# A decoder trunk on one core: the start's transfers divided between SyncE's and ScalarE's queues

## The reference

```python
c_act = jax.nn.silu(c)
for l in range(DEPTH):
    mod = c_act @ ada_w[l] + ada_b[l]
    sh1, sc1, g1, sh2, sc2, g2 = [t[:, None, :] for t in jnp.split(mod, 6, axis=-1)]
    h = rms_norm(x, norm_mix_w[l]) * (1.0 + sc1) + sh1
    proj = h @ w_in[l]
    ...            # window attention and mLSTM branches, gates, conv, merge
    x = x + g1 * (merged @ w_out[l])
    h2 = rms_norm(x, norm_ffn_w[l]) * (1.0 + sc2) + sh2
    x = x + g2 * grouped_moe(h2, router_w, router_bias, w_gate[l], w_up[l], w_down[l])
return x
```

## Time and profile before

| what | value |
|---|---|
| median of three executions | 1733.24 us |
| profiled execution, first to last instruction (span) | 1724.8 us |
| median less span (what lies around the span, and differences between executions) | 8.4 us |
| TensorE busy | 1506.9 us, 87% of the span |
| first matmul record | 11.38 us |
| head on TensorE | 18.40 to 44.06 us |
| last transfer of the head landed | 38.62 us |
| bytes moved | 366.59 MB, mean 213 GB/s |

### The profile page before, as it was taken

One profiled execution on the slowest core, in us unless ns is written; L12 is line 12 of the kernel. 1 busy time (PEld: TensorE's weight loads), 2 busy tenths in 40 slices (PEclk: granted clock), 3 DMA queues, 4 the chain that ended last, 5 costly groups with the idle time before them and its releaser, 6 DMA issues.

```text
span 1724.8 us, 18335 instructions
## 1 busy us (share of the span) xinstructions
PE 1506.9 (87%) x5819; PEld 669.3 (39%) x5820; DVE 563.9 (33%) x1459; ACT 323.4 (19%) x809; POOL 121.8 (7%) x157
## 2 busy tenths in 40 slices
PE   4999999999983999987749999999999387999982
PEld 1544444544441333332335444454444132333330
DVE  1346432446333212111134554243642411221213
ACT  3133411200011212111132343111000121221210
POOL 1100000011101000000111000000110100000001
PEclk8999999999996999999769999999999789999996
DMA  9822111055747899999952111113563799997984
GB/s 307 338 97 98 49 49 49 13 206 173 291 142 268 268 375 379 376 388 360 322 180 98 49 49 50 49 49 108 206 224 145 292 314 381 378 354 247 310 303 165
DMA packets 160813, 366.59 MB, mean 213 GB/s; under 512 B 12433, under 2 KB 14705, under 8 KB 160753
## 3 DMA queue, kind: packets, MB, share of 16 engines
q1 hardware_dynamic: 127568, 256.26, 42.2%
q0 software_dynamic: 21664, 83.89, 12.8%
q10 hardware_dynamic: 11520, 25.70, 5.0%
HBM read 334.37 MB, written 31.46 MB: 212 GB/s over the span
## 4 chain that ended last, share of the span: by engine, by line
PE 69%; DMA 11%; SPq 5%; DVE 5%; issue 4%; ACT 2%; POOL 2%; ACTq 0%; DVEq 0%; POOLq 0%; PEldq 0%
PE bank L939 23%; PE bank L1160 14%; PE bank L929 11%; PE bank L1105 6%; PE bank L1172 6%; DMA weight_ring<-in_w_up_dram 6%; DMA regA<-in_w_up_dram 2%; SPq L428 2%; SPq L431 2%; SPq L371 2%; DMA weight_ring<-in_ada_w_dram 1%; PE bank L1152 1%; PE bank L999 1%; POOL expert_rows L558 1%; PE bank L988 1%
## 5 line engine op out<-in xcount | busy, mean ns | idle before, releaser
L939 PE MATMUL bank<-h_features,weight_ring 128*128 128x512 f32 x768 | 342.4, 599 | 3.1 <-ACT regB L674 1.9
L1160 PE MATMUL bank<-weight_ring,merged_features 128*64 128x512 f32 x960 | 227.2, 628 | 35.3 <-DMA weight_ring<-in_w_up_dram 28.2
L939 PEld LDWEIGHTS bank<-h_features,weight_ring 128*128 128x128 f32 x768 | 144.8, 192 | 182.7 <-issue 182.4
L929 PE MATMUL bank<-weight_ring,h_features 128*128 128x512 f32 (+1 forms) x512 | 196.1, 541 | 1.7 <-ACT h_features L628 1.7
L1703 DVE TENSOR_TENSOR merged_features<-bank,merged_features 64x512 f32<-64x512 f32 x44 | 30.5, 693 | 381.8 <-ACT merged_features L809 381.8
L1160 PEld LDWEIGHTS bank<-weight_ring,merged_features 128*64 128x64 f32 x960 | 73.5, 144 | 165.4 <-issue 160.8
L929 PEld LDWEIGHTS bank<-weight_ring,h_features 128*128 128x128 f32 x512 | 96.0, 190 | 97.0 <-issue 91.6
L1160 PE MATMUL bank<-h_features,merged_features 128*64 128x512 f32 x256 | 117.1, 612 | 11.0 <-DMA regA<-in_w_up_dram 10.0
L1160 PE MATMUL bank<-regA,merged_features 128*64 128x512 f32 x256 | 117.5, 614 | 0.0
L1105 PE MATMUL bank<-weight_ring,merged_features 128*128 128x512 f32 x256 | 110.4, 593 | 3.0 <-POOL merged_features L538 3.0
L1172 PE MATMUL bank<-weight_ring,merged_features 128*64 128x512 f32 x480 | 109.6, 598 | 1.6 <-DVE merged_features L1689 1.6
(11 more groups left out here) (304 smaller groups left out, 1376.1 us busy)
## 6 DMA issues: line engine op xcount, KB each, us to landing
weight_ring<-in_ada_w_dram SPq DMA_DIRECT2D x24, 2048.0 KB, 8.7
weight_ring<-in_w_gate_dram SPq DMA_DIRECT2D x22, 2048.0 KB, 21.1
weight_ring<-in_w_down_dram POOLq DMA_DIRECT2D x22, 2048.0 KB, 14.9
weight_ring<-in_w_up_dram SPq DMA_DIRECT2D x22, 2048.0 KB, 20.4
weight_ring<-in_w_in_dram SPq DMA_DIRECT2D x18, 2048.0 KB, 8.9
h_features<-in_w_gate_dram SPq DMA_DIRECT2D x10, 2048.0 KB, 17.4
regA<-in_w_up_dram SPq DMA_DIRECT2D x10, 2048.0 KB, 27.4
regB<-in_w_down_dram POOLq DMA_DIRECT2D x10, 1536.0 KB, 11.5
```

The lines of the kernel that those rows point to most:

```text
L929: ins = te.matmul(bank[:, 0:w], hT[:, k, P * i:P * i + P], wv[:, k, :], start=(k == 0), stop=(k == KD - 1))
L939: ins = te.matmul(bank[:, :], wv[:, k, c0:c0 + P], rhs[:, k, :], start=(k == 0), stop=(k == kn - 1))
L1160: ins = te.matmul(ps[3][64 * part:64 * part + 64, :], xT[:, k, :], w[:, k, :], start=(k == 0), stop=(k == KD - 1))
```

## The change

SP issues `c`, the positions and then all four conditioning pieces in a row. The tokens, the router bias, the router matrix and the fourteen parameter transfers are issued by ScalarE, ahead of its first activation, in that order; the wait for `zeroed` goes with them. `params` now takes the engine as an argument; in the second layer's case SP issues them as before. Nothing that any engine waits for is changed, and no byte is added or removed.

```diff
+        def params(eng, l):
+
+            def rows(dst, src):
+                eng.dma_start(dst, src).then_inc(params_in, 16)
...
         @block.sync
         def _(sp):
-            def params(l):
...
             sp.dma_start(crow, c.rearrange("a (k p) -> (a k) p", p=P)).then_inc(const_in, 16)
             with nc.allow_non_contiguous_dma(reason="positions by token"):
                 sp.dma_start(rt[:, 0:NT].bitcast(I32), positions.rearrange("a (i p) -> p (a i)", p=P)).then_inc(const_in, 16)
-            sp.dma_start(rbias[:, :], router_bias.rearrange("(a e) -> a e", a=1).to_broadcast([P, E])).then_inc(const_in, 16)
-            load_item(sp, 0, 0, head_in[0])
-            sp.wait_ge(zeroed, 2)
-            sp.dma_start(rwz[:, :, 0:E], router_w.rearrange("(k p) e -> p k e", p=P)).then_inc(const_in, 16)
-            params(0)
-            sp.dma_start(xs[:, :, :], x.rearrange("a (i p) d -> p (a i) d", p=P)).then_inc(x_in, 16)
-            for n in range(1, HEAD):
+            for n in range(HEAD):
                 load_item(sp, 0, n, head_in[n])
...
                 with sp.If(l < DEPTH - 1):
-                    params(nxt)
+                    params(sp, nxt)
...
             ac = nc.scalar

+            act.dma_start(xs[:, :, :], x.rearrange("a (i p) d -> p (a i) d", p=P)).then_inc(x_in, 16)
+            act.dma_start(rbias[:, :], router_bias.rearrange("(a e) -> a e", a=1).to_broadcast([P, E])).then_inc(const_in, 16)
+            act.wait_ge(zeroed, 2)
+            act.dma_start(rwz[:, :, 0:E], router_w.rearrange("(k p) e -> p k e", p=P)).then_inc(const_in, 16)
+            params(act, 0)
             act.wait_ge(dve_const, 1)
```

More of the change, by code:

```diff
@@ L361, in share @@
             return cleared[n::5]
+        def params(eng, l):
+            def rows(dst, src):
+                eng.dma_start(dst, src).then_inc(params_in, 16)
+            rows(prm[0:8, :], lay(norm_mix_w, l).rearrange("a (k p) -> (a k) p", p=P))
+            rows(prm[8:16, :], lay(norm_ffn_w, l).rearrange("a (k p) -> (a k) p", p=P))
+            rows(prm[16:48, :], lay(conv_w, l).rearrange("a j (m p) -> (a j m) p", p=P))
+            rows(prm[48:56, :], lay(conv_b, l).rearrange("a (m p) -> (a m) p", p=P))
+            rows(prm[56:60, :], lay(mlstm_norm_w, l).rearrange("a (m p) -> (a m) p", p=P))
+            rows(prm[60:108, :], lay(ada_b, l).rearrange("a (m p) -> (a m) p", p=P))
+            rows(g1bc[:, :], lay(ada_b, l)[:, 2 * D:3 * D].to_broadcast([P, D]))
+            rows(wqk[:, 0, :], lay(q_norm_w, l).to_broadcast([P, HD]))
+            rows(wqk[:, 1, :], lay(k_norm_w, l).to_broadcast([P, HD]))
+            rows(sinkb[:, :], lay(sinks, l).to_broadcast([P, HQ]))
+            with nc.allow_non_contiguous_dma(reason="gate columns and biases"):
+                rows(gbias[0:4, :], lay(b_igate, l).rearrange("a h -> h a"))
+                rows(gbias[32:36, :], lay(b_fgate, l).rearrange("a h -> h a"))
+                rows(wgz[:, :, 0:4], cols8(w_in, l, MI, 4))
+                rows(wgz[:, :, 4:8], cols8(w_in, l, MF, 4))
         block = ctx.enter_context(nc.Block())
```

## The result

The changed kernel is slower, by less than forecast. Median 1735.12 us (1730.96 to 1739.41, 20 runs) against 1731.38 us (1725.11 to 1740.47, 20 runs) before; the ratio is 1.0024, with a 95% interval of 1.0013 to 1.0035. By the ratio that is +4.2 us (2.3 to 6.1) where +10.6 was forecast; the medians differ by 3.7. The time lies inside the stated range and the change has the forecast sign, but it is within the 0.3% that was to count as no change, and less than half of what was forecast. Of the 8.7 us between the forecast time (1743.8) and the median, 1.9 come from the kernel before, whose median of three was 1733.24. In what follows, one of the eight executions of experiment 4 is left out of every figure: it took 2701.77 us at a mean granted clock of 0.56.

The account below looks back on a forecast made before the run. Bound at the start by three paths ending together (pieces 1 and 3, token path), then dense TensorE work. Parameters at 34.3 plus a 20.35 us head end at 54.65 against 44.06: +10.6 on 1733.24 gives 1743.8 us, range 1729 to 1749.

Parts of the forecast that it names:

- Turns between queues: SP's and ScalarE's queues at the start: one packet each in turn, so 259 turns put parameters at 34.3 us; chance 0.62.
- The first phase: Start of the queues: `x` goes in turn with the positions' 4-byte packets, 5.5 us, and its packets are over at 7.9.
- The head's own time: TensorE from parameter transpose to last conditioning sum: dense from 34.3, 20.35 us, end at 54.65 against 44.06 before.
- Three paths that end together: Start of the kernel before: pieces 1 and 3 and the token path end together, then TensorE runs 12.76 us nearly without gap.
- ScalarE's hold: ScalarE held while issuing, let go at 24 us with about 105 packets per engine standing; hidden with 2 us to spare.
- Median less span: Whole kernel: the 8.4 us between profiled span and median time is carried along unchanged into the forecast.
- The chances: Whole kernel against a 0.3% (5.2 us) threshold: slower 0.64, same 0.31, faster 0.05.
- rival of small packets several to a turn: Queues at the start: 1.6 to 2.5 small packets per 2 KB piece, parameters at 26.4 to 21.6, +2.7 to -2.0 us; chance 0.24.
- n = 1.25: Small packets per 2 KB piece at about which the loss was said to pass 0.3%.
- rival of turns slower than their packets: Queues at the start: a turn takes 1.38 times its packets' time, +20 us, 1754 us; chance 0.05.

Follow-up runs that it names:

- experiment 4: Kernel before, but TensorE starts the head only when all four conditioning pieces have landed, transfers unchanged; 1739.34 us, ratio 1.0047 to the kernel before.
- experiment 6: Changed kernel, but SP issues the four conditioning pieces only when ScalarE's parameters have landed; 1734.34 us, ratio 1.0005 to the kernel before.
- experiment 3: Changed kernel, but SP issues the gate columns behind the four pieces, with their own count; 1732.87 us, ratio 1.0008 to the kernel before.
- experiment 1: Kernel before, but only `x` is issued from ScalarE, everything else stays with SP; 1729.48 us, ratio 0.9981 to the kernel before.
- experiment 2: Changed kernel, but `x` is issued by SP behind piece 0, only the small transfers by ScalarE; 1730.34 us, ratio 0.9980 to the kernel before.
- experiment 5: Kernel before, but TensorE repeats conditioning group 0 five times and group 2 twice, transfers unchanged; 1734.15 us, ratio 1.0007 to the kernel before.
- experiment 7: Changed kernel, but SP issues everything in one queue, gate columns, router bias and router matrix last with own counts; 1727.80 us, ratio 0.9974 to the kernel before.

## Why the prediction was right and wrong

**Turns between queues: right where it was needed.** Small packets of one queue and 2 KB packets of the other pass one for one, at 92 ns a pair where 94 were reckoned; predicted were parameters at 34.3 and the router matrix at 15.7, measured 35.5 and 17.4. Experiment 6 takes the neighbour away and the same transfers land 20 us earlier; experiment 3 takes 130 of the packets away and the head starts 11 us earlier. The first phase was read too simply: beside `x` the positions' 4-byte packets did not go in turn (12 of them passed with 197 of `x` between 4 and 6 us), and some still passed when `x` was over. The rest of the 1.2 and 1.7 us is not taken apart.

**The head's own time: wrong, and this is the step that failed.** "From 34.3 TensorE runs the head dense: ... 20.35 us". The mechanism, a dense head from the landing of the parameters, was right; its size was taken from rows at 1.2 GHz. It measured 13.3 us. The text had seen that the clock might be the higher one and priced that at 3.4 us less, from group 0's 3.21 us "at 1.00". That row was misread. The first clock record in the trace of the kernel before begins at 21.44 us, and ahead of it the column shows 1.00 for want of a record; group 0 ran from 18.81 to 22.02, mostly at the lower level, and a group at 2.4 GHz is 1.92. The terms add up: 10.6 + 1.2 (later parameters) - 7.0 (shorter head) is the +4.8 us measured at the head's end. Experiment 4 shows the short head without any change of transfers: 13.7 us.

**Three paths that end together: right,** and it has a second side. Before, TensorE stood about 5.7 us within the head, for pieces 1 and 3 and for ScalarE; these waits and the lower clock of most of its groups make the 12.3 us between 25.7 and 13.3. The late start of the changed kernel removes both, all but the first two groups' share. Experiment 3 shows that the paths stand close: with the parameters out of the way the first sum waits for ScalarE.

**ScalarE's hold: right in sign,** too long by 5 us, no cost. When ScalarE was let go at 18.7 us, 2308 of its packets were still to pass, 144 on each engine, where the estimate was 105.

**Median less span.** The 8.4 us stand alike in the time before and in the forecast time, so they did not touch the forecast change. One execution's time less its own span is 1.6 us (1737.23 less 1735.6; 1726.02 less 1724.4). The rest was that the profiled execution of before was a fast one.

**The chances.** 0.64 for slower by over 0.3% rested on the whole 10.6. With the head 7.0 us shorter the same sum gives +3.6, under the stated bound of 5.2 us, and "no change" would have been the likelier. The rival of small packets several to a turn, whose places were taken as mixed evidence, is refuted by 1733 to 1732 and by parameters at 35.5 where it had 21.6 to 26.4. Its turning point, n = 1.25, was a slip: by the prediction's own terms a loss of 5.2 us is reached at about n = 1.35. The rival of turns slower than their packets is refuted by the 92 ns a pair.

Open is why experiments 1, 2, 5 and 7 time 2.5 to 4 us better than the first projection of their one profile stands against the mean of before. For experiment 7 it is 1.9 us ahead, and 4.5 us (2.1 to 6.9) were measured; its last projection of the first layer starts at 441.77, only 0.2 us ahead of that mean. So the profile does not show where the timed gain of experiment 7 lies.

## What to carry to other kernels

In these runs a transfer of thousands of tiny pieces was cheap alone (about 10 ns a packet and engine) and dear beside 2 KB pieces (92 ns), because the two queues took turns by packets: moved to a queue of its own it landed later, and so did whatever waited for it. Of the two remedies tried, letting such transfers pass first and alone (experiment 6) came out level with the kernel before, and putting them behind everything that is waited for, with a count of their own (experiment 7), came out 0.3% ahead. When a wait goes or comes in front of TensorE, price the matmuls behind it at the clock they will have there, from rows at both levels, not at the one they had.

## What the runs showed of the hardware

- In the three profiles of the kernel before, one group of 16 matmul records of 512 columns, 32 rows each, takes 3.21 to 3.64 us at 1.2 GHz or mostly so, and 1.92 at 2.4 (second profile); a sum of eight one-column matmuls takes 1.86 and 1.05. In every head here the first groups take more than 1.92 us each.
- Waits of TensorE of 2.0, 2.5 and 2.8 us (experiments 5, 3 and 6) were followed by the lower level, waits of 1.8 and 1.9 us (experiments 7 and 6) by a group of 1.92. A shorter wait was no warrant: the third profile of before has 1.54 us and then a group of 3.32. What decides it is not shown.
- The clock column reads 1.00 ahead of the first clock record of a trace, and that tells nothing of the clock. The first record begins at 21.44 us in the first profile of before and at 39.49 us in that of the changed kernel, both near the end of the head's first group.

```profile
19.00:22.60 3.60, 3.60 (x17) 0.59 (x16) 0.00 (x0) 0.68 (x1) 0.00 (x0) 1.00 1.02 407
38.80:40.70 1.90, 1.86 (x17) 0.43 (x17) 0.00 (x0) 0.00 (x0) 0.00 (x0) 1.00 1.04 348
```

These are two stretches of the second profile of before (busy PE, PEld, DVE, ACT, POOL, PEclk, DMA share, GB/s): group 0 and group 3, the same work, 3.64 and 1.92 us, both under 1.00.

- An issuing engine is let go long before its packets have passed: ScalarE issued its last transfer by 18.7 us, and the last landed at 35.4.
